# Three products of rounded halves for the attention scores, with half of x parked in DRAM

## The reference, cut to what matters

```python
q = (q * cos + rotate_half(q) * sin) * (DIFF_HEAD_DIM ** -0.5)
k = k * cos + rotate_half(k) * sin
...
for qb in range(seq // Q_BLOCK):
    s0, s1 = qb * Q_BLOCK, (qb + 1) * Q_BLOCK
    scores = jnp.einsum('bhmqd,bhmkd->bhmqk', q[:, :, :, s0:s1], k[:, :, :, :s1],
                        preferred_element_type=jnp.float32)
    mask = chunk_id[s0:s1, None] >= chunk_id[None, :s1]
    p = jax.nn.softmax(jnp.where(mask, scores, NEG_INF), axis=-1)
    attn = p[:, :, 0] - lam * p[:, :, 1]
    outs.append(jnp.einsum('bhqk,bhkd->bhqd', attn.astype(v.dtype), v[:, :, :s1]))
...
x = layer_norm(DN_ALPHA * x + y, mix_ln_g[layer], mix_ln_b[layer])
```

## Time and profile before

| | |
|---|---|
| median of 3 runs | 3737.18 us (3728.3 to 3741.58) |
| the profiled execution | 3731.83 us, its span 3729.9 us |
| granted TensorE clock over the span | 0.968 |
| TensorE busy (matmul) | 3549.0 us, 95% |
| VectorE, ScalarE, GpSimd busy | 1820.0, 1209.0, 518.9 us |
| attention, heads 0 to 7 | from 1171 to 1680 us of the span |

### The profile page before, as it was taken

The page is one execution under the profiler, slowest core; times in us unless marked ns, Lnnn a source line. Parts: engine busy times, 40 slices in busy tenths (PEclk is TensorE's granted clock), DMA queues, the critical chain, the costliest instruction groups (busy, mean ns, idle before and its releaser), DMA issues. The chain is left out here.

```text
span 3729.9 us, 41262 instructions
## 1 busy us (share of the span) xinstructions
PE 3549.0 (95%) x15892; PEld 2837.0 (76%) x15892; DVE 1820.0 (49%) x2311; ACT 1209.0 (32%) x1741; POOL 518.9 (14%) x287
## 2 busy tenths in 40 slices
PE   8979999999998999969999999999978899999997
PEld 6758888888876777737888888888866678888886
DVE  7986423233255666655423233554567774323235
ACT  4245411111144444454411112445342352202123
POOL 0015200000051000026100000443001540000004
PEclk9999999999999999989999999999977999999998
DMA  2102213122122111102213123222221222111112
GB/s 102 34 34 74 96 62 106 46 85 78 49 91 61 44 57 39 51 6 89 92 58 106 45 91 105 94 93 91 86 68 46 68 84 94 49 51 45 46 61 96
DMA packets 75277, 258.52 MB, mean 69 GB/s; under 512 B 10144, under 2 KB 10528, under 8 KB 75168
## 3 DMA queue, kind: packets, MB, share of 16 engines
q1 hardware_dynamic: 75168, 257.07, 21.4%
HBM read 243.92 MB, written 4.72 MB: 67 GB/s over the span
## 5 line engine op out<-in xcount | busy, mean ns | idle before, releaser
L197 PE MATMUL ps<-xh,whi 128*128 128x512 f32 x2816 | 982.0, 394 | 43.6 <-DVE wlo L180 18.7
L197 PE MATMUL ps<-xl,whi 128*128 128x512 f32 x2816 | 974.0, 391 | 0.0
L197 PE MATMUL ps<-xh,wlo 128*128 128x512 f32 x2816 | 973.3, 391 | 0.0
L180 DVE TENSOR_TENSOR wlo<-stage,whi 128x1024 fp32r<-128x1024 f32 x361 | 518.4, 1436 | 492.2 <-ACT whi L174 491.1
L174 ACT ACTIVATE whi<-stage 128x1024 fp32r<-128x1024 f32 x361 | 381.2, 1056 | 1065.4 <-PE ps L197 1031.5
L197 PEld LDWEIGHTS ps<-xh,whi 128*128 128x128 f32 x2816 | 532.0, 189 | 162.5 <-issue 30.5
L197 PEld LDWEIGHTS ps<-xh,wlo 128*128 128x128 f32 x2816 | 532.0, 189 | 111.6
L197 PEld LDWEIGHTS ps<-xl,whi 128*128 128x128 f32 x2816 | 532.4, 189 | 109.7
L197 PE MATMUL ps<-hh,whi 128*128 128x512 f32 x1216 | 422.5, 396 | 6.0 <-ACT lam_t L2068 3.9
L197 PE MATMUL ps<-hl,whi 128*128 128x512 f32 x1216 | 421.3, 395 | 0.0
L197 PE MATMUL ps<-hh,wlo 128*128 128x512 f32 x1216 | 421.3, 395 | 0.0
(11 more groups left out here) (375 smaller groups left out, 3830.0 us busy)
## 6 DMA issues: line engine op xcount, KB each, us to landing
stage<-in_w_ff SPq DMA_DIRECT2D x88, 512.0 KB, 3.5
stage<-in_w_gate SPq DMA_DIRECT2D x59, 512.0 KB, 3.2
stage<-in_w_up SPq DMA_DIRECT2D x59, 512.0 KB, 3.2
stage<-in_w_in SPq DMA_DIRECT2D x50, 512.0 KB, 3.2
ada<-in_w_ada SPq DMA_DIRECT2D x48, 512.0 KB, 3.3
stage<-in_w_qkv SPq DMA_DIRECT2D x43, 512.0 KB, 3.3
stage<-in_w_down SPq DMA_DIRECT2D x48, 448.0 KB, 3.3
stage<-in_w_out SPq DMA_DIRECT2D x32, 512.0 KB, 3.3
```

The source lines that it names most:

```text
L180: dve.tensor_tensor(wlo[slot][:], stage[slot][:], whi[slot][:].bitcast(F32), ALU.subtract).then_inc(w_split, 1)
L197: done = pe.matmul(acc[:, h * HALF:(h + 1) * HALF], wt[slot][:, w], xt[:, b, h * HALF:(h + 1) * HALF], start=b == 0 and wt is whi and xt i ...
```

## The change

The rotated sum is now kept as a high and a low part, and the scores are three float32r products per map and chunk, map 0 and map 1 in turn. For heads 1 to 7 ScalarE makes the high part at tiles 4 and 7 and GpSimd the low part; for head 0 VectorE makes both. The low parts need 16 KB per partition, which are taken from blocks 4 to 7 of x: these 2 MB are stored to DRAM after the norm before attention and loaded again in two parts, the first after the scores of head 6, the second after the scores of head 7. The loads of the output projection's units from 4 on are queued behind.

```diff
+    X_AT = -(-nc.sbuf_base // 32) * 32
...
+    turned = [[at_kb(f"turned{k}{n}", [P, S], 40 + 8 * k + 4 * n) for n in range(2)] for k in range(2)]
+    rot_hi = [[at_kb(f"rot_hi{k}{n}", [P, S], 40 + 8 * k + 4 * n, F32R) for n in range(2)] for k in range(2)]
+    rot_lo = [[nc.alloc_sbuf_tensor_at(f"rot_lo{k}{n}", [P, S], F32R, offset=X_AT + (4 + 2 * n + k) * 4 * S) for n in range(2)] for k in range(2)]
+    rot_lo_first = [at_kb(f"rot_lo_first{k}", [P, S], 24 + 4 * k, F32R) for k in range(2)]
+    x_away = nc.dram_tensor("x_away", (P, DB // 2, S), F32).ap()
...
# first_rope, VectorE, per half of q and of k of head 0
-        dve.tensor_tensor(dst, dst, half(swp, k), ALU.add).then_inc(done, 1)
+        dve.tensor_tensor(half(swp, k), dst, half(swp, k), ALU.add).then_inc(total, 1)
+        dve.wait_ge(total, at + k + 1)
+        dve.tensor_copy(hi, half(swp, k)).then_inc(high, 1)
+        dve.wait_ge(high, high_at + k + 1)
+        dve.tensor_tensor(half(rot_lo_first[k], h), half(swp, k), hi.bitcast(F32), ALU.subtract).then_inc(done, 1)
...
# head_raw, ScalarE
             act.wait_ge(mm_done, u + 3)
+            act.wait_ge(rope_done, head.n(2, min(k, 1)))
         if k:
-            act.wait_ge(rope_done, head.n(2, k))
+            act.wait_ge(rope_sum, ROPE_SUM + head.n(2, k))
...
# head_rope, VectorE
-        dve.tensor_tensor(dst[:], dst[:], swp[:], ALU.add).then_inc(rope_done, 1)
+        dve.tensor_tensor(swp[:], dst[:], swp[:], ALU.add).then_inc(rope_sum, 1)
+
+    def head_rope_hi(act, head, k):
+        act.wait_ge(rope_sum, ROPE_SUM + head.n(2, k + 1))
+        act.activation(rot_hi[k][head.par][:], swp[:], ACT.Copy).then_inc(rope_hi, 1)
+
+    def head_rope_lo(pool, head, k):
+        pool.wait_ge(rope_hi, ROPE_HI + head.n(2, k + 1))
+        pool.tensor_tensor(rot_lo[k][head.par][:], swp[:], rot_hi[k][head.par][:].bitcast(F32), ALU.subtract).then_inc(rope_done, 1)
...
# scores, TensorE
-            for m in range(2):
-                f = slice(m * HEAD_DIM, (m + 1) * HEAD_DIM)
-                done = pe.matmul(pS[m][:, at:at + n], q_rot[head.par][f, qt * P:(qt + 1) * P],
-                                 k_rot[head.par][f, at:at + n], start=True, stop=True)
+            for q, kk in ((q_hi, k_hi), (q_hi, k_lo), (q_lo, k_hi)):
+                for m in range(2):
+                    f = slice(m * HEAD_DIM, (m + 1) * HEAD_DIM)
+                    done = pe.matmul(pS[m][:, at:at + n], q[f, qt * P:(qt + 1) * P], kk[f, at:at + n],
+                                     start=q is q_hi and kk is k_hi, stop=q is q_lo)
...
# act_head, before the raw copies of the tile
+            if project and qt in (4, 7):
+                head_rope_hi(act, nxt, (4, 7).index(qt))
...
# SyncE
             project(Head(0))
+            sp.wait_ge(*fn0[1].done(DB - 1))
+            sp.dma_start(x_away, x[:, DB // 2:DB, :]).then_inc(x_out, 16)
             project(Head(1))
...
+            for u in range(2, 4):
+                load(sp, o1a, 0, u)
+            for n in range(2):
+                sp.wait_ge(sc_done, NT * (HEADS - 1 + n))
+                sp.dma_start(x[:, 4 + 2 * n:6 + 2 * n, :], x_away[:, 2 * n:2 * n + 2, :]).then_inc(x_back, 16)
+            for u in range(4, o1a.n):
+                load(sp, o1a, 0, u)
...
# VectorE, residual of the output projection
+                if u in (4, 6):
+                    dve.wait_ge(x_back, X_BACK + 8 * u - 16)
...
# GpSimd, before the low parts of the finished heads
+            pool.wait_ge(x_out, X_OUT + 16)
+            pool.wait_ge(*fn0[1].split_done(DB - 1))
+            all_heads(pool, pool_head)
```

More of the change, by code:

```diff
@@ L1180, in program @@
     swp = at_kb("swp", [P, S], 36)
-    q_rot = [at_kb(f"q_rot{k}", [P, S], 40 + 4 * k) for k in range(2)]
-    k_rot = [at_kb(f"k_rot{k}", [P, S], 48 + 4 * k) for k in range(2)]
+    turned = [[at_kb(f"turned{k}{n}", [P, S], 40 + 8 * k + 4 * n) for n in range(2)] for k in range(2)]
[3 more added lines that the diff above has]
+    x_away = nc.dram_tensor("x_away", (P, DB // 2, S), F32).ap()
     e1 = at_kb("e1", [P, S], 56)
@@ L1193, in program @@
          "swapped0", "rope0_a", "rope0_b", "rope0_done")]
+    rope_sum, ROPE_SUM, rope_hi, ROPE_HI = lru_m, 4 * AB, lru_v, 3 * AB
+    rope0_sum, ROPE0_SUM, rope0_hi, ROPE0_HI = gates, 2 * AB, decays, 2 * AB
+    x_out, X_OUT, x_back, X_BACK = wg_in, 64, sp_step, 3
     gqa, gq = plan["qkva"], plan["qkv"]
@@ L1224, in first_rope @@
         a, b, done, moved = ((rope0_a, rope0_b, rope0_done, swapped0), (rope_a, rope_b, rope_done, swapped))[h]
-        dst = half((q_rot, k_rot)[k][0], h)
+        total, at, high, high_at = ((rope0_sum, ROPE0_SUM, rope0_hi, ROPE0_HI), (rope_sum, ROPE_SUM, rope_hi, ROPE_HI))[h]
+        dst, hi = half(turned[k][0], h), half(rot_hi[k][0], h)
         dve.wait_ge(acc_free, g.base + k + 3)
@@ L1317, in head_rope @@
         u, _, _ = head.unit(k)
-        dst = (q_rot, k_rot)[k][head.par]
+        dst = turned[k][head.par]
         dve.wait_ge(acc_free, u + 3)
@@ L1342, in scores @@
             pe.wait_ge(exp1, head.n(NT, qt))
+        (q_hi, k_hi), (q_lo, k_lo) = [(r[0][head.par], r[1][head.par]) for r in (rot_hi, rot_lo)]
+        if head.is_first:
+            q_lo, k_lo = rot_lo_first
         for at in range(0, w, HALF):
             n = min(HALF, w - at)
-            for m in range(2):
-                f = slice(m * HEAD_DIM, (m + 1) * HEAD_DIM)
-                done = pe.matmul(pS[m][:, at:at + n], q_rot[head.par][f, qt * P:(qt + 1) * P],
-                                 k_rot[head.par][f, at:at + n], start=True, stop=True)
+            for q, kk in ((q_hi, k_hi), (q_hi, k_lo), (q_lo, k_hi)):
[3 more added lines that the diff above has]
+                                     start=q is q_hi and kk is k_hi, stop=q is q_lo)
         done.then_inc(sc_done, 1)
@@ L1497, in dve_head, with pool_head @@
                                      ALU.mult, ALU.subtract).then_inc(attn, 1)
+    def pool_head(pool, head, before, project):
+        for k in range(2):
+            head_rope_lo(pool, head.next(), k)
     def all_heads(eng, run):
@@ L1956, in _ @@
             sp.dma_start(c_row[:], io["c_rows"]).then_inc(c_in, 16)
-            for g in (o1a, o1b, f1.a, f1.b):
+            for u in range(2, 4):
[5 more added lines that the diff above has]
+                load(sp, o1a, 0, u)
+            for u in range(2):
+                load(sp, o1b, 0, u)
+            for g in (o1b, f1.a, f1.b):
                 alternating(sp, g)
```

## The result

The changed kernel takes 3755.23 us (median of 7 runs, 3754.34 to 3761.22), the kernel before 3732.8 us (7 runs, 3728.3 to 3741.58). The ratio is 1.0056, with a 95% interval of 1.0044 to 1.0068. By that ratio the change costs some 21 us. The prediction said 3734 and no difference that can be measured.

What follows compares the result with a forecast made beforehand. TensorE, busy 95% of the span, was taken as the bound. Heads 0 to 6 give -3.7 us, the last head -0.3, the first +1.2: -2.8, so 3729.0, or 3734 against the median; range 3721 to 3756.

Steps and rivals of the forecast that it cites:

- (c): Attention, GpSimd forms the low parts, 2.82 us per op; k's leaves 1.0 us of slack, so no cost.
- (D): GpSimd and VectorE get in each other's way in attention: at most 1 us a head, 3741 us; chance 0.12.
- (a): Tile 7: weighted products wait for ScalarE's last copy, so the 0.32 us saved turns into a longer wait.
- (b): ScalarE's added copies: at tile 4 exponentials move 0.77 us and 0.22 is lost; at tile 7 nothing.
- The products: Attention scores: three rounded products per map and chunk save 1.07 us a middle head, 0.53 of it net.
- B: Score pairs do not overlap, six steps in place of three: 5.6 us a head more, 3775 us; chance 0.12.
- C: Narrow score chunks or issue are dearer: +0.9 us a head, 3748 us, half-way 3741; chance 0.16.
- The first head: Head 0's VectorE rope: half ropes gain a copy and a subtraction; only the fourth is on the path, +1.2 us.
- The last head: Head 7: the scores' saving counts only at tile 7, where VectorE waits for scores: 0.3 us gained.
- Part 2, x in DRAM: Store of 2 MB takes 13 to 19 us, each 1 MB fetch 9; no cost unless 1 MB takes over 15.

Runs made afterwards that it cites:

- low_quarters: Changed kernel with each low part formed by four GpSimd operations of 128x256 in place of one of 128x1024: 3742.52 us, ratio 1.0006 to the kernel before.
- late_low: Changed kernel with GpSimd's low part of k waiting until VectorE has written tile 7's bias: 3738.16 us, ratio 0.9999 to the kernel before.
- late_f32: late_low with one f32 matmul of the high parts per map and chunk, low parts formed but unused: 3738.57 us, ratio 1.0000.
- the reordered pair: late_low with ScalarE's last weight copy earlier at tiles 5 and 7, with three products or one f32: ratios 0.9968 (again 0.9963) and 0.9997.
- before_x_away: Kernel before with only the store of half of x to DRAM and its loads back: 3733.31 us against 3740.9, ratio 0.9987.

## Why the prediction was wrong

**The step that failed** is (c) of part 1, the low part in GpSimd, where it "now has nothing to do", priced at nothing for VectorE; and with it rival (D), which had the right mechanism and the wrong victim. Step (c) asked only who waits for the low part, and there it was right: 2.38 us, over before the next scores. It did not ask what VectorE does beside it. (D) did, but looked for VectorE's long operations, the rescaling, and for where their slack lies. It passed over the shortest operation, the bias, whose end releases both exponentials. In the timeline of VectorE before, the bias of tile 7 ends just where ScalarE goes on at 1401.74:

```profile
1401.54 0.17 DVE L1482 TENSOR_SCALAR nb<-mx 128x2 f32<-128x2 f32 x1
```

Step (c) itself put the high part at "about 1401.5", so GpSimd's start and the bias were bound to meet within a fraction of a microsecond. In the changed kernel GpSimd began 0.25 us ahead of it, and nearly its whole operation was still to come. The "up to 2.1 lost per GpSimd op" of (D) was in fact lost in full, 2.0 us in each of seven heads. Priced like this, (D) would have given 14 us for the waits where it had at most 7.

**What no step held** is the other part of the loss. The sum moved TensorE's idle time and never asked what a longer idle time does to its clock. At the ends of heads 0 to 6, waits of 0.59 to 1.21 us at this place left 1.00 in the next 3 us, with one exception (low_quarters at the end of head 6, 0.63 behind 1.17). Behind waits of 1.95 to 2.03 it was 0.58 to 0.69, once 1.00, and behind 2.83 to 2.86 it was 0.50 to 0.59. That is the 1.6 us at the start of every head from head 1 on. So the length of the wait goes with the lower clock, but doesn't decide it alone.

**(a) and (b), the places where ScalarE limits.** Tile 7: the wait was to grow from 0.62 to 0.9, and in late_low, where the contention is gone, it is 0.87. Tile 4: the exponential was to come 0.77 late. It starts at 1393.57, 0.69 after the bias ends (1392.88). From tile 4's first scores to tile 5's it is 7.10 us, 7.00 before, though tile 4's scores save 0.10: 0.2 are lost, as summed. Both right. One reading beside them was off: the 7.7 us in 16 waits reach into the last head; heads 0 to 6 alone have 6.4 us in 14.

**The products** were to save 1.07 us a head, 0.53 of it kept. With ScalarE's wait still there late_low's head 3 is 0.58 us shorter than before. Added up over the eight tiles of head 3, it is 9.49 us from a tile's first score matmul to the next other matmul in late_f32 and 8.27 in late_low: 1.2 a head, of which heads 1 to 6 keep 0.7. In the reordered pair they keep (347.7 - 342.3) / 6 = 0.9. The term is right, a little low, and most of it is to be had once ScalarE is out of the way. Narrow pairs start every 0.06 to 0.16 us, where 0.119 a step was taken; so a chunk of 128 columns costs 0.06 us more than before, not 0.14. The page "TensorE: Matmul & The Clock Gate" of the Trainium skill (section "Wait — 56ns, not 53.3ns?") gives some 62 ns for each matmul when hardware decoding is off. By that a narrow pair could not start in less than 0.124; the rows of tile 4 have 0.06 and 0.11, so that bound is not in force here. Rivals B and C fell with these rows.

**The first head** was to cost 1.2 us. VectorE's timeline of the changed kernel, last half rope:

```profile
1174.90 0.43 DVE L1242 CAST rot_hi<-swp 128x512 fp32r<-128x512 f32 x1
1175.36 0.69 DVE L1244 TENSOR_TENSOR rot_lo_first<-swp,rot_hi 128x512 fp32r<-128x512 f32 x1
```

TensorE then starts after 8.36 us of waiting, 7.29 before: 1.1 more.

**The last head** was to gain 0.3. In late_low it is 0.3 us longer than before. Between the scores of tiles 5 and 6 it loses 0.8 (17.20 against 16.41), where two matmuls of the sums of squares take 2.08 us instead of 1.12, at a granted clock of 0.50 instead of 1.00; the other tiles together gain 0.5. Both kernels waited 2.9 us just ahead of those two matmuls, and before the clock came down too, but about 1.4 us behind the end of the wait. What sets that moment stays open.

**Part 2, x in DRAM.** The DMA issues of the changed kernel (KB each, us to landing):

```profile
x_away<-x SPq DMA_DIRECT2D x1, 2048.0 KB, 8.6
...
x<-x_away SPq DMA_DIRECT2D x2, 1024.0 KB, 5.2
```

They are faster than the 13 to 19 and the 9 us that were taken, and before_x_away shows no cost. Right in what it said of the time, with sizes that were too large.

**The numbers.** 3755.23 lies within the range of 3721 to 3756, at its very end, and that is luck: the upper end came from (C), dearer narrow chunks, which did not happen. The chances stood on "no difference" for 0.70. (D) had 0.12 at 3741, of which 0.02 counted for a time above 3748.

## What to carry to other kernels

Before work is given to idle GpSimd, list what VectorE starts while it runs, the tiniest operations first: each can grow to the length of the GpSimd instruction, and what counts is who waits for it, not its size. Put GpSimd behind such an operation with a wait of its own, or cut its instruction. Where a wait of TensorE grows to the 2 us or more seen here, count the clock of the microseconds behind it as well; and where the end of a chain on ScalarE limits, try its order too, since part of a saving on TensorE shows only when that wait is gone.

## What the runs showed of the hardware

A VectorE tensor_scalar of 128x2 that starts after a GpSimd subtraction has begun ends with the GpSimd instruction: 2.17 us beside 2.38, 1.50 beside 1.89, 0.51 beside the first of four pieces, 0.73 long, each time up to 0.04 us after GpSimd's own end, and 0.17 alone. A reciprocal of the same size inside a GpSimd subtraction of 2.38 stays at 0.17. The page "SBUF — State Buffer" of the Trainium skill (section "Who interferes with whom") says that VectorE in a two-port mode, which tensor_scalar can enter, and GpSimd share a port pair that whoever issues first keeps for the whole instruction, and that VectorE instructions outside these modes with at most one input in SBUF do not contend. The four durations and the reciprocal agree with that; that the bias ran in such a mode is inferred, not shown.

Matmuls on the two halves of TensorE's rows ran side by side in either order in which they stood in the program: with map 0's three products of a chunk ahead of map 1's, the records still come in pairs of the same product, every 0.23 us for 512 columns, as when they are issued in turn. (The records do not say which of a pair is which map.)

GpSimd's subtraction of 128x1024 takes 2.38 us with two different inputs, 1.89 with one input twice and an f32 output, and 2.80 in four pieces.
